# Stick-breaking attention: the next item's first score row, its sigmoids and its scan ahead of the current item's transposes and chunk copies

## The reference

```python
def block(args):
    qb, t0 = args
    t = t0 + jnp.arange(Q_BLOCK)
    mask = key_pos[None, :] < t[:, None]
    z = jnp.einsum("bhqd,bhkd->bhqk", qb, kf) * scale
    log_keep = jnp.where(mask, jax.nn.log_sigmoid(-z), 0.0)
    later = lax.cumsum(log_keep, axis=3, reverse=True) - log_keep
    log_a = jax.nn.log_sigmoid(z) + later
    a = jnp.where(mask, jnp.exp(log_a), 0.0)
    return jnp.einsum("bhqk,bhkd->bhqd", a, vf)
```

## Time and profile before

| | us |
|---|---|
| median of 3 runs (2813.9 to 2817.59) | 2815.68 |
| the profiled execution | 2814.47 |
| its span | 2812.8 |
| TensorE busy in the span | 2671.0 |
| VectorE / ScalarE / GpSimd busy | 1442.4 / 1052.2 / 521.7 |

### The profile page before, as it was taken

One profiled execution on the slowest core, in us unless ns is written; L12 is line 12 of the kernel. 1 busy time (PEld: TensorE's weight loads), 2 busy tenths in 40 slices (PEclk: granted clock), 3 DMA queues, 4 the chain that ended last, 5 costly groups with the idle time before them and its releaser, 6 DMA issues. The chain is left out here.

```text
span 2812.8 us, 35231 instructions
## 1 busy us (share of the span) xinstructions
PE 2671.0 (95%) x12704; PEld 2224.0 (79%) x12704; DVE 1442.4 (51%) x1773; ACT 1052.2 (37%) x1719; POOL 521.7 (19%) x425
## 2 busy tenths in 40 slices
PE   7999999989999999999989999996998999999999
PEld 7888888878888878887877777775787888887887
DVE  6454444176444542324677777777327644444131
ACT  6451012144333330215656666664323433333020
POOL 2200000102322310003033333332010322221000
PEclk8999999999999999999999999998999999999999
DMA  6401111122223261114101111111312232226111
GB/s 203 142 31 45 45 52 49 49 90 105 89 97 104 82 229 47 49 36 135 61 22 31 30 30 30 30 30 62 127 52 90 98 104 94 93 82 232 51 52 70
DMA packets 57414, 221.44 MB, mean 79 GB/s; under 512 B 7280, under 2 KB 7280, under 8 KB 52080
## 3 DMA queue, kind: packets, MB, share of 16 engines
q1 hardware_dynamic: 43920, 164.68, 17.6%
q0 software_dynamic: 13120, 49.29, 5.1%
q10 hardware_dynamic: 288, 6.29, 0.5%
HBM read 170.43 MB, written 49.81 MB: 78 GB/s over the span
## 5 line engine op out<-in xcount | busy, mean ns | idle before, releaser
L1760 PE MATMUL ps<-xg_hi,w_hi 128*128 128x512 f32 x1344 | 542.8, 404 | 37.9 <-DVE up L1218 16.8
L1762 PE MATMUL ps<-xg_hi,w_lo 128*128 128x512 f32 x1344 | 529.3, 394 | 0.0
L1761 PE MATMUL ps<-xg_lo,w_hi 128*128 128x512 f32 x1344 | 528.9, 394 | 0.0
L1760 PE MATMUL ps<-tile_hi,g_hi 128*128 128x512 f32 x1064 | 419.6, 394 | 12.6 <-DVE up L1686 12.4
L1762 PE MATMUL ps<-tile_hi,g_lo 128*128 128x512 f32 x1064 | 417.5, 392 | 0.0
L1761 PE MATMUL ps<-tile_lo,g_hi 128*128 128x512 f32 x1064 | 415.5, 391 | 0.0
L1760 PEld LDWEIGHTS ps<-xg_hi,w_hi 128*128 128x128 f32 x1344 | 255.9, 190 | 94.9 <-issue 26.4
L1762 PEld LDWEIGHTS ps<-xg_hi,w_lo 128*128 128x128 f32 x1344 | 255.2, 190 | 55.9
L1761 PEld LDWEIGHTS ps<-xg_lo,w_hi 128*128 128x128 f32 x1344 | 256.3, 191 | 47.2 <-issue 0.7
L1760 PE MATMUL ps<-act_hi,d_hi 128*128 128x512 f32 x704 | 276.7, 393 | 0.0
L1762 PE MATMUL ps<-act_hi,d_lo 128*128 128x512 f32 x704 | 275.6, 392 | 0.0
(11 more groups left out here) (211 smaller groups left out, 4127.1 us busy)
## 6 DMA issues: line engine op xcount, KB each, us to landing
raw<-wpack SPq DMA_DIRECT2D x108, 512.0 KB, 3.6
quads<-wpack SPq DMA_DIRECT2D x38, 1024.0 KB, 5.5
d_raw<-wpack SPq DMA_DIRECT2D x32, 704.0 KB, 4.2
stage<-d_act POOLq DMA_DIRECT2D x44, 512.0 KB, 6.6
d_act<-up SPq DMA_DIRECT2D x38, 256.0 KB, 2.1
d_act<-gate SPq DMA_DIRECT2D x38, 256.0 KB, 2.2
d_x<-x SPq DMA_DIRECT2D x16, 512.0 KB, 6.4
x<-d_x SPq DMA_DIRECT2D x16, 512.0 KB, 4.8
```

Source lines behind the costliest of these rows:

```text
L1760: pe.matmul(out, whi, mhi, start=start, stop=False, skip_group_check=chained)
L1761: pe.matmul(out, whi, mlo, start=False, stop=False, skip_group_check=chained)
L1762: return pe.matmul(out, wlo, mhi, start=False, stop=stop, skip_group_check=chained)
```

## The change

In each item the order is changed on three engines. On TensorE, row 0 of the next item (`z`) stands first, then the transposes of the first two chunks, then the filler behind row 0, row 1 and so on as before. On ScalarE, the two sigmoids of row 0 stand before the copies of the first two chunks, and the sigmoids of row 1 after them. On VectorE, the scan of row 0 stands before the residuals of the first two chunks, which stand before `finished(0)` (the copy to tf) and the scan of row 1. The waits go with their instructions. GpSimd's and SyncE's lists are unchanged. The last item of the last pair has no next item and keeps its order.

```diff
--- before.py
+++ after.py
@@ -960,11 +960,12 @@
 
                         for it in range(ITEMS):
                             t, hh = it % 4, it // 4
-                            for c in range(min(t + 1, 2)):
-                                chunk(hp, it, c, first)
-                            if not (last and it == ITEMS - 1):
-                                for r in range(2):
+                            for r in range(2):
+                                if not (last and it == ITEMS - 1):
                                     sigmoids(hp * ROWS + (2 * (it + 1) + r), (it + 1) % 2, r, (it + 1) % 4)
+                                if r == 0:
+                                    for c in range(min(t + 1, 2)):
+                                        chunk(hp, it, c, first)
                             if not last and it in (0, 3, 7):
                                 prep(u0 + 5 + (it + 1) // 4, hp * 3, hp)
                             if not last and it in (4, 5):
@@ -1474,12 +1475,16 @@
                                 if not last and (it, n) in ENDS:
                                     project(hp + 1, ENDS[it, n])
 
-                            for c in range(min(t + 1, 2)):
-                                chunk(hp, it, c)
+                            if last and it == ITEMS - 1:
+                                for c in range(min(t + 1, 2)):
+                                    chunk(hp, it, c)
                             if not (last and it == ITEMS - 1):
                                 for r in range(2):
                                     row, n = hp * ROWS + (2 * (it + 1) + r), key_count(r, (it + 1) % 4)
                                     scan(row, (it + 1) % 2, r, (it + 1) % 4)
+                                    if r == 0:
+                                        for c in range(min(t + 1, 2)):
+                                            chunk(hp, it, c)
                                     if last and r == 1:
                                         dve.wait_ge(scanned, row + 1)
                                         dve.wait_ge(sig_ready, row + 1)
@@ -2062,8 +2067,6 @@
 
                         for it in range(ITEMS):
                             t = it % 4
-                            for c in range(min(t + 1, 2)):
-                                turn(hp, it, c, par, first)
                             if it == ITEMS - 1 and first:
                                 pe.wait_ge(zeros_made, 3)
                             if it == ITEMS - 1 and not last:
@@ -2075,6 +2078,9 @@
                                       False)
                                 elif not last:
                                     z(hp * ROWS + (ROWS + r), 1 - par, 0, r, 0, False)
+                                if r == 0:
+                                    for c in range(min(t + 1, 2)):
+                                        turn(hp, it, c, par, first)
                                 fill(FILL[it][r])
                             if it == 0:
                                 pe.wait_ge(vT_lo_ready, hp * 2 + 2)
```

## The result

The changed kernel takes 2795.22 us (median of 4 runs, 2793.56 to 2796.37), the kernel before in the same comparison 2815.61 us: ratio 0.9927, 95% interval 0.9912 to 0.9941, 20.4 us less. The forecast was 2795. In a second comparison it took 2794.54 against 2815.32 (0.9925, interval 0.9908 to 0.9943).

A forecast was written before the change was run, and what follows sets the result against it. TensorE, busy 2671.0 of 2812.8 us, bounds the kernel, so only its gaps can be won. Gains of 10.5 (filled pairs) and 10.8 (last pair), 21.3 us off the 2815.68 median, give 2795 us, range 2785 to 2809.

The forecast's parts named there:

- Filled pairs: Seven head pairs with filler projections: 1.5 us gained per pair, 10.5 us in all, bounds 0 and 3.9 per pair.
- Item 1: Filled pairs: 0 gained; the 0.57 us wait leaves the transposes but returns at the filler behind score row 1.
- F1: Filler behind score row 1 in filled pairs; forecast to stay at 1564.9 in item 1 and come 0.2 later in item 2.
- Item 2: Filled pairs: filler behind score row 1 0.2 us later, scan row 1 2.29, third weighted sum not waiting, end at 1579.45.
- Item 3: Filled pairs: row 0 fits before transposes at 1580.0, first weighted sum waits 0.5 us; total 0.45 gained at its end.
- Scans of row 1: VectorE in filled pairs: 768 columns in 1.75 us, not 2.23; 1024 in 2.29, not 2.72; last pair's 2.2.
- Last pair: Pair without filler: 10.8 us gained, bounds 5 and 15; items 2 and 6 3.0 each, item 1 2.4, item 5 1.7.
- The shared port: VectorE and GpSimd instructions with two SBUF inputs lock each other out; without this rule some 14 us gain, not 21.
- (a): Rival: filled pairs give nothing, each wait taken from the transposes returns at the filler; 2805 us, chance 0.14.
- (b): Rival: all transpose waits vanish, 7 x 3.9 + 11.9 = 39 us, 2777 us; chance 0.06 with other times below 2786.
- (c): Rival: residuals before tf delay the filler in items 1, 2, 5, 6 unless scan r0 starts earlier; 2822 us, chance 0.07.
- (d): Rival: last pair's gains are half and items 2 and 5 lose; 2812 us, no measurable change, chance 0.11.

The follow-up runs named there:

- e7: Changed kernel with GpSimd's product of row 0 cut to 2 columns: 2791.71 us, ratio 0.9916 to the kernel before.
- e1: New order on all three engines in the last pair alone, filled pairs as in the kernel before: 2803.10 us against 2816.06, ratio 0.9954.
- e2: New order on all three engines in the seven filled pairs alone, last pair as in the kernel before: 2806.63 us, ratio 0.9966.
- e4: New order on TensorE and ScalarE, VectorE as in the kernel before: 2852.69 us, ratio 1.0131 to the kernel before.
- e5: New order on ScalarE and VectorE, TensorE as in the kernel before: 2846.08 us, ratio 1.0113 to the kernel before.
- e9: New order on TensorE and VectorE, ScalarE as in the kernel before: 2869.52 us, ratio 1.0187 to the kernel before.
- e3: New order on TensorE alone, ScalarE and VectorE as in the kernel before: 2803.91 us, ratio 0.9955 to the kernel before.
- e8: Changed kernel with VectorE's copy to tf moved directly behind the scan of row 0, before the residuals: 2778.09 us, ratio 0.987 to the kernel before.
- e10: Kernel before with only VectorE's copy to tf moved, behind the residuals and before both scans: 2871.55 us, ratio 1.0213 to the kernel before.

## Why the prediction was right, point by point

- **Total**: 21.3 forecast, 20.4 measured. The mechanism held, but that the sum came out within 1 us is in part luck: below, errors of up to 1.9 us cancel.
- **Filled pairs**: 1.5 a pair forecast, 1.43 measured, with the path as described: transposes' waits 3.9 to 0.4 ("under 1.2"), tf waits 1.9 to 3.9 ("about 4"). Cumulated over the items of a pair, the forecast gain was 0 (item 1), 0.45 (end of 3), 0.5 (5), 0.9 (6), 1.55 (7); measured in one pair are 0.2, 0.24, 0.8, 0.9 and 1.47.
- **Item 1**: "the wait only moves to F1". It does (0.72 to 1.28), and the item gains 0.2, not 0.
- **Item 2**: F1 was to come 0.2 later. It does: it starts 6.78 us behind the last matmul of item 1, before 6.61, with a wait of 0.97 (0.45 before). What follows F1 is 0.48 shorter, since the third weighted sum no longer waits, and the item as a whole gained 0.37; forecast was 0.2.
- **Item 3**: forecast 0.2 of gain beyond item 2's; measured 0.33 of loss (8.80 to 9.13). The term for the first weighted sum's wait was right in size (0.43 for 0.5). Left out were what came behind it: VectorE's weight conversion met GpSimd's product of row 1 (1.70, not 1.23 us, and 1.70 in e7 too, which cuts row 0's product alone), and the third weighted sum waited 0.15. From start to start these two waits cost 0.60 and 0.32, more than the brackets say.
- **Scans of row 1**: 1.74 and 2.29 against 1.75 and 2.29 in the filled pairs. In the last pair the one of 1024 was put at 2.2 and took 2.90.
- **Last pair**: 10.8 forecast, 10.4 measured, from terms that missed in both directions. Item 2 gained 3.95 and item 6 3.6, not 3.0; item 1 2.0 and not 2.4, item 5 2.2 and not 1.7. Item 3 lost 1.2 (6.30 to 7.48) where 0.7 for items 3, 4 and 7 together was booked as a gain. The residual of chunk 2, behind the product, ends item 2, and the next row and transposes run at a granted clock of 0.58 between 1918.8 and 1926 us. Over the whole of item 3 the clock was 0.88 before, 0.82 in e1 and 0.76 after, for 6.30, 6.89 and 7.48 us: the prediction had no term for it.
- **The shared port**: "some 14 in place of 21" without it, given without its working, puts it at 7. With row 0's product cut in both kernels the change brings 13.6 us, so some 7 are right as a sum. But in the last pair it is only 1.4 (5.1 before, 3.7 after), since GpSimd's product now meets scan row 1.
- **Rivals**: (a), no gain in the filled pairs, falls by e2. (b), all waits vanish, falls by the tf waits. (c) was near in its mechanism, though the residuals stood in front of tf before the change too: e4, e5 and e9 have such a scan, one that does not start early enough, and cost 31 to 54 us and not 6. The 7% that I gave to it fitted only because all three engines were moved. (d), half the gain in the last pair, falls by the length of that pair.
- **What I had wrong beside it**: the share of TensorE's own move, which I put at 4 us before e3. By e3 it brings 12 of the 20 us.

## What to carry to other kernels

When work is pulled ahead across engines, move every link of the chain, and walk each engine's string from the producer: with the same instructions, two of three links moved cost 31 to 54 us here, the first alone (TensorE's) saved 12 and all three 20. After a wait has moved, look at what ends it now. Here it was one copy behind two residuals that nobody needed yet, and moving it was worth almost as much as the whole change (16 us), but only on top of it: in the old order, in front of both scans, it cost 56.

## What the runs showed of the hardware

- A wait costs more than its length once the clock falls with it. Filled pairs whose longest waits are up to 1.4 us had a granted clock of 1.00 (after, e3, e8); those with waits of 1.8 to 2.4 us (e4, e5, e9, e10) showed 0.93 to 0.98, and in one pair of e4 the same matmuls took 2.9 us more busy time. The length of the wait alone does not decide: a wait of 2.12 us in e4 left the clock at 1.00, and in the last pair the transposes behind 1.0 us ran slow in one kernel and not in the other.
- VectorE and GpSimd, when both read two SBUF operands, hold each other up, and the one that began goes through: GpSimd's 895 columns took 3.67 us behind a scan and 1.76 when they began first, and then the scan took 2.90 and not 2.27. Residuals, which read one operand from PSUM, and GpSimd's product did not slow each other (two residuals in 1.25 us beside the product of 1.76).
